# Weight loads of two blocks instead of four in a hybrid attention and FFN layer on one core

## The reference

```python
h = rmsnorm(x, attn_norm)
qkv = einsum('bsd,de->bse', h, w_in).reshape(B, S, 3, 16, 64)
q, k, v = rope(qkv[:, :, 0]), rope(qkv[:, :, 1]), qkv[:, :, 2]
o_moba = moba_attention(q[:, :, :8], k[:, :, :8], v[:, :, :8])      # 256 rows are one block: plain causal
o_dil  = dilated_mixture(q[:, :, 8:], k[:, :, 8:], v[:, :, 8:])     # windows 128/1, 512/4, 2048/16
mixed = concat([rmsnorm(o_moba, g1), rmsnorm(o_dil, g2)])
x = x + mixed @ w_out
h = rmsnorm(x, ffn_norm)
x = x + (silu(h @ w_gate) * (h @ w_up)) @ w_down                     # 1024 -> 2816 -> 1024
out = rmsnorm(x, final_norm)
```

## Time and profile before

| | |
|---|---|
| median of three runs | 304.27 us (304.18 to 304.38) |
| the profiled execution | 304.51 us |
| its span, first to last instruction | 302.7 us |
| TensorE busy | 294.1 us, 97% of the span |
| VectorE, ScalarE busy | 203.7 us, 166.9 us |
| granted TensorE clock | 0.994 of full speed |
| ring loads | 47 of 1 MB, 4.8 us from issue to landing (median) |
| DMA engines busy in the main queue | 57.5% |

### The profile page before, as it was taken

The page is one execution under the profiler, slowest core; times in us unless marked ns, Lnnn a source line. Parts: engine busy times, 40 slices in busy tenths (PEclk is TensorE's granted clock), DMA queues, the critical chain, the costliest instruction groups (busy, mean ns, idle before and its releaser), DMA issues.

```text
span 302.7 us, 4335 instructions
## 1 busy us (share of the span) xinstructions
PE 294.1 (97%) x1448; PEld 240.0 (79%) x1448; DVE 203.7 (67%) x332; ACT 166.9 (55%) x283; POOL 19.3 (6%) x29
## 2 busy tenths in 40 slices
PE   8999999999999899999999999999999999999992
PEld 4688877887788688888888888888888888888882
DVE  3889999977898589729755555637465655455454
ACT  4877775829686549816554445354363545444224
POOL 0011000030333120200000000000000000000010
PEclk9999999999999999999999999999999999999997
DMA  7998445851695535765876566575656564651003
GB/s 255 422 423 302 178 178 141 266 140 79 172 372 177 187 135 150 277 236 210 269 266 207 226 186 264 173 241 174 207 176 249 174 267 159 238 200 28 0 0 139
DMA packets 21757, 61.65 MB, mean 204 GB/s; under 512 B 2545, under 2 KB 13809, under 8 KB 15601
## 3 DMA queue, kind: packets, MB, share of 16 engines
q1 hardware_dynamic: 21312, 60.70, 57.5%
q10 hardware_dynamic: 432, 0.80, 0.7%
HBM read 54.67 MB, written 1.05 MB: 184 GB/s over the span
## 4 chain that ended last, share of the span: by engine, by line
PE 82%; ACT 5%; DMA 5%; issue 3%; DVE 2%; SPq 2%; POOL 0%; POOLq 0%; ACTq 0%; DVEq 0%
PE bank L437 27%; PE bank L439 26%; PE bank L438 26%; DMA raw<-in_weights 2%; DMA room<-in_first 2%; ACT w_hi L725 1%; SPq L403 1%; DMA room<-room 1%; ACT probs L820 1%; PE bank L464 1%; ACT vals L793 1%; PE bank L447 1%; DVE xs L1152 0%; ACT o_hi L836 0%; DVE w_lo L939 0%
## 5 line engine op out<-in xcount | busy, mean ns | idle before, releaser
L725 ACT ACTIVATE w_hi<-raw 128x1024 fp32r<-128x1024 f32 x94 | 98.0, 1056 | 81.2 <-PE bank L439 72.2
L939 DVE TENSOR_TENSOR w_lo<-raw,w_hi 128x1024 fp32r<-128x1024 f32 x94 | 112.3, 1217 | 17.1 <-ACT w_hi L725 15.7
L437 PE MATMUL bank<-w_hi,x_hi 128*128 128x512 f32 x270 | 106.8, 396 | 0.6 <-DVE w_lo L967 0.6
L439 PE MATMUL bank<-w_hi,x_lo 128*128 128x512 f32 x270 | 105.2, 390 | 0.0
L438 PE MATMUL bank<-w_lo,x_hi 128*128 128x512 f32 x270 | 105.2, 390 | 0.0
L437 PEld LDWEIGHTS bank<-w_hi,x_hi 128*128 128x128 f32 x270 | 50.7, 188 | 12.3 <-DVE w_lo L967 1.4
L439 PEld LDWEIGHTS bank<-w_hi,x_lo 128*128 128x128 f32 x270 | 50.7, 188 | 10.6
L438 PEld LDWEIGHTS bank<-w_lo,x_hi 128*128 128x128 f32 x270 | 50.7, 188 | 10.1
L437 PE MATMUL bank<-w_hi,h_hi 128*128 128x512 f32 (+1 forms) x82 | 31.6, 385 | 0.0
L439 PE MATMUL bank<-w_hi,h_lo 128*128 128x512 f32 (+1 forms) x82 | 31.5, 384 | 0.0
L438 PE MATMUL bank<-w_lo,h_hi 128*128 128x512 f32 (+1 forms) x82 | 31.5, 384 | 0.0
(11 more groups left out here) (101 smaller groups left out, 245.6 us busy)
## 6 DMA issues: line engine op xcount, KB each, us to landing
raw<-in_weights SPq DMA_DIRECT2D x47, 1024.0 KB, 4.8
room<-room SPq DMA_DIRECT2D x88, 64.0 KB, 2.1
room<-in_first SPq DMA_DIRECT2D x3, 384.0 KB, 5.1
room<-in_first SPq DMA_DIRECT2D x1, 1024.0 KB, 7.5
xs<-in_x SPq DMA_DIRECT2D x2, 512.0 KB, 9.3
out<-rot SPq DMA_DIRECT2D x3, 256.0 KB, 2.0
room<-in_first SPq DMA_DIRECT2D x1, 640.0 KB, 8.6
vals<-in_final_norm ACTq DMA_DIRECT2D x1, 512.0 KB, 7.2
```

What stands on the lines that cost most here:

```text
L437: pe.matmul(dst, a_hi, w1, start=first, stop=False)
L439: return pe.matmul(dst, a_lo, w1, start=False, stop=last)
L725: act.activation(w_hi[:, slot:slot + 2, :], raw[:, slot:slot + 2, :], ACT.Copy).then_inc(hi_ready, 1)
L939: dve.tensor_tensor(w_lo[:, slot:slot + 2, :], raw[:, slot:slot + 2, :], w_hi[:, slot:slot + 2, :].bitcast(f32), ALU.subtract).then_inc(lo ...
```

## The change

`quad` becomes `pair`: each load brings two blocks, 512 KB, as 128 rows of 4 KB that lie 8 KB apart in memory. There are six semaphores `raw_full`, one for each pair of slots. SP issues a pair when VectorE has finished with its own two slots: the first half waits for one `lo_ready` less than the quad did, the second half for the same count as the quad. The 47 ring loads become 94. The places of the other DMAs between them stay, behind both halves. The last loads of the six at the start no longer count on a semaphore of the ring but on their own. `split_hi` waits for the pair's semaphore, with the number of loads worked out by `ring_loads` (slots of the first four pairs have had one load fewer, since the first eight blocks don't pass through `raw`).

```diff
-        raw_full = [sem(f"raw_full{i}") for i in range(NQ)]
+        raw_full = [sem(f"raw_full{i}") for i in range(RING // 2)]
...
-        in_first = [raw_full[blocks[-1] // QUAD] if blocks[-1] % QUAD == QUAD - 1 else sem(f"in_first{i}")
-                    for i, (row_blocks, blocks) in enumerate(FIRST_LOADS)]
+        in_first = [sem(f"in_first{i}") for i in range(len(FIRST_LOADS))]
...
-            def quad(q, pos):
-                sp.dma_start(raw[:, pos * QUAD:(pos + 1) * QUAD, :].rearrange("p b n -> p (b n)"),
-                             weights[bass.ds(q - FIRST_QUADS, 1), :, :].rearrange("q p n -> (q p) n")).then_inc(raw_full[pos], 16)
+            def pair(q, pos, h):
+                first = 2 * h
+                sp.dma_start(raw[:, pos * QUAD + first:pos * QUAD + first + 2, :].rearrange("p b n -> p (b n)"),
+                             weights[bass.ds(q - FIRST_QUADS, 1), :, first * NB:(first + 2) * NB]
+                             .rearrange("q p n -> (q p) n")).then_inc(raw_full[2 * pos + h], 16)
...
-            quad(2, 2)
+            pair(2, 2, 0)
+            pair(2, 2, 1)
             sp.dma_start(tab[:, 0:C_MASK], table[:, 0:C_MASK]).then_inc(in_tab, 16)
-            sp.wait_ge(lo_ready, 2)
-            quad(NQ, 0)
+            for h in range(2):
+                sp.wait_ge(lo_ready, h + 1)
+                pair(NQ, 0, h)
...
             def ring_quad(r, pos):
-                sp.wait_ge(lo_ready, r * (RING // 2) + (2 * pos + 2 - RING // 2))
-                quad(r * NQ + pos, pos)
+                for h in range(2):
+                    sp.wait_ge(lo_ready, r * (RING // 2) + (2 * pos + h + 1 - RING // 2))
+                    pair(r * NQ + pos, pos, h)
...
             for q in range(BLOCKS // RING * NQ, BLOCKS // QUAD):
-                sp.wait_ge(lo_ready, 2 * q - 4)
-                quad(q, q % NQ)
+                for h in range(2):
+                    sp.wait_ge(lo_ready, 2 * q + h - 5)
+                    pair(q, q % NQ, h)
...
+            def ring_loads(p):
+
+                return 16 * (p // (RING // 2) + (0 if p % (RING // 2) < SINGLES // 2 else 1))
...
             def split_pair(p):
-                q = p // 2
-                if p < RING // 2:
-                    split_hi(2 * p, q, 16, None)
-                else:
-                    split_hi(2 * p % RING, q % NQ, 16 * (q // NQ + 1), 2 * p - 10)
+                split_hi(2 * p % RING, p % (RING // 2), ring_loads(p), 2 * p - 10 if p >= RING // 2 else None)
...
-                        q = (HI0 + m) // 2
-                        split_hi(2 * (HI0 + m) % RING, q % NQ, c * 16 + 16 * (q // NQ),
+                        p = HI0 + m
+                        split_hi(2 * p % RING, p % (RING // 2), c * 16 + (ring_loads(p) - 16),
                                  c * STEP_BLOCKS + (2 * (HI0 + m) - 10 - STEP_BLOCKS))
```

More of the change, by code:

```diff
@@ L378, in _ @@
             for pos in range(1, NQ):
-                sp.wait_ge(lo_ready, 2 * pos + 2)
-                quad(NQ + pos, pos)
+                for h in range(2):
+                    sp.wait_ge(lo_ready, 2 * pos + h + 1)
+                    pair(NQ + pos, pos, h)
             sp.dma_start(tab[:, C_MASK:C_END], table[:, C_MASK:C_END]).then_inc(in_mask, 16)
             def ring_quad(r, pos):
-                sp.wait_ge(lo_ready, r * (RING // 2) + (2 * pos + 2 - RING // 2))
-                quad(r * NQ + pos, pos)
+                for h in range(2):
+                    sp.wait_ge(lo_ready, r * (RING // 2) + (2 * pos + h + 1 - RING // 2))
+                    pair(r * NQ + pos, pos, h)
             def place_squares(c):
@@ L717, in _, with split_hi @@
             act.activation(warm_out[:, 0:1], warm[:, 0:1], ACT.Exp)
-            def split_hi(slot, pos, quad_round, done):
-                if quad_round is not None:
-                    act.wait_ge(raw_full[pos], quad_round)
+            def ring_loads(p):
+                return 16 * (p // (RING // 2) + (0 if p % (RING // 2) < SINGLES // 2 else 1))
+            def split_hi(slot, pos, loads, done):
+                act.wait_ge(raw_full[pos], loads)
                 if done is not None:
```

## The result

The changed kernel takes 305.18 us, the median of 12 runs from 304.27 to 306.54, against 304.27 us before (12 runs, 304.08 to 304.82). The ratio is 1.0031, with a 95% interval of 1.0019 to 1.0042: slower by 0.9 us, beyond the forecast's range. The runs also spread three times as far, though the kernel before itself later spread from 303.78 to 305.44 on another chip (35 runs).

The account below looks back on a forecast made before the run. TensorE, busy 294.1 of 302.7 us, was taken as the bound. Start, loop, issue and VectorE counted 0 and rows ahead of tile 11 +0.1, so 304.27 became 304.4 us, with a range of 303.7 to 305.0.

Parts of the forecast that it names:

- the bound and the place: TensorE bounds the kernel; the change comes near only its 0.92 us wait at `values` of tiles 10 and 11.
- The packets: Ring loads ahead of tile 11: shorter rows cost 0.08 us a quad, between 0 and 0.25, counted as +0.1 us.
- Half a load lands sooner: Ring loads: 512 KB lands in 2.9 us; ScalarE's longest load wait ends some 2 us sooner, worth 0 at tile 10.
- 47 more DMA instructions: SP's issue of DMAs: hidden in its waits, 0 to +0.65 us later at tile 11's issue.
- a later issue of tile 11 is hidden by a shorter landing: Tile 11's last placement DMA: time behind the ring load hides up to 1.86 us of later issue; counted 0, at most 0.65.
- VectorE: VectorE's work before tile 10: disturbed moves might give back or lose 0.7 us; taken at 0.
- rival B: Wait at 100.9 us shrinks as placements pass sooner or VectorE regains 0.7 us: 303.7 us, chance 0.10.
- Rival A: SP between 93.96 and 97.5 us: tile 11's DMAs go out and end 0.65 us later; 305.0 us, chance 0.16.
- `values` past 101.5: Sign of a slower kernel: `values` of tiles 10 and 11 start later than 101.5 us, against 100.92 before.
- Rival C: Ring loads in the loop stop overlapping, each paying its fixed part: 65 us more, 370 us, chance 0.01.

Follow-up runs that it names:

- the changed kernel again: The changed kernel with nothing altered, run once more for a second profile: two runs, 305.64 and 307.14 us.

## Why the prediction was wrong

Right were the bound and the place. TensorE waits three times, nowhere for a split from the ring; the FFN loop turn stays at 16.3 us; ScalarE's waits for loads fall from 8.8 to 2.6 us, though those for TensorE rise only from 72.2 to 73.0, where as much was forecast as the others fall; tile 11 is the exposed spot. What failed is how much reaches it.

*The step "The packets" failed.* It had a row cost its bytes plus 0.010 us, +0.1 us for a quad, from placements whose source is on the chip, and let that go straight to tile 11. As engine time the term was within its bound of 0.25: by the shares of the main queue, 57.5% of 302.7 us before and 60.2% of 303.6 after, the 47 quads cost 8.7 us more, 0.19 each, and by 58.6% of 302.8 us for 4 KB rows in one DMA 0.07 each. But what reaches TensorE is the landing, and there the runs showed something that the sum had no term for: the source address. Tile 11's last DMA lands in 4.47 us in place of 3.86, +0.6 us where +0.1 stood. Of that the contiguous pairs alone would have made -0.8 (3.08 us), and the stride +1.4. The two loads of (5, 1) tell it in each profile: the second half lands 4.5 to 4.6 us after its issue when contiguous, 5.3 to 6.6 when strided. From 95 to 98 us strided pairs move 184 to 257 GB/s, contiguous ones 295 and 302, whole loads of 1 MB 235 to 283. Bounds on a kind of read that the trace doesn't have should have been wider.

*The step "Half a load lands sooner" failed in size.* A straight line from 2.0 to 4.8 us gave 2.9; measured is 5.2, outside both ends. ScalarE's wait ended at 83.2 us, not near 82. The 2.0 us were those of a store of another kind, and the median in the queue includes what stands ahead.

*The step "47 more DMA instructions" was half right.* Its tally of the pushes, 0.65, 1.3 and 1.95 us, left 1.3 us of SP's pause. It took an issue as 0.63 us whatever the queue holds. With six DMAs where there were five, tile 8's took 1.0 us longer, the longest one 1.32 us, and the pause was gone. Kernels with the added DMAs around tile 8 all show this to a degree, from 2.73 us (contiguous pairs, tile 11 first) over 3.10 (the changed kernel again) to 4.52 (only (5, 1) whole), and whole loads there give 2.49 to 2.52; by what limit the issue is held back was not tried. That a later issue of tile 11 is hidden by a shorter landing, as the prediction had it, came out for half a us in both profiles of the added DMAs with hardly any bytes. Behind strided pairs it did not: in the second profile of the changed kernel 0.7 us came on top of a landing of 4.60.

*VectorE* did win time back, as rival B had it: tile 10 was turned at 91.0 us (90.30 + 0.70), 0.5 sooner once the shift of the start is taken off. It was worth nothing, since SP was busy until 91.4.

Rival A named the right place and half of the cause. In the first profile tile 11 was not issued later, it landed later; in the second it was both. Its price of +0.75 us and 305.0 us is close to what came, in part by luck, since the stride wasn't in it, and its test, `values` past 101.5, was met. It deserved more than 0.16: a place with no slack, a change that touches the queue ahead of it, and two unmeasured prices, both of which could only go one way by much. Rival C did not happen as a whole: pairs overlap, and the loop hides their slowness.

Left open: why strided loads land later though the engines are busy no longer, and why the profile with padding between the rows doesn't show it at tile 11; why contiguous pairs are faster than a quad (0.9983 against 1, and 1.0005 for the quad of 4 KB rows); the 0.6 us that the median of the kernel with tiny added DMAs shows and its profiles don't; and that with (3, 1) to (4, 0) in pairs besides (5, 1) the time is 305.05 (1.0024) and without them 304.74 (1.0008), whose intervals overlap.

## What to carry to other kernels

Before cutting a load in two, ask what each half reads: halves by columns of a row-major piece read with gaps, and the layout in memory should be cut along with the load. Where one queue carries both bulk loads and small transfers that an engine waits for, find the small transfer with no slack and put it ahead of the load; that was worth 0.7 us here (304.33 to 303.58) and needed nothing else. Slack between DMA issues in a trace is no promise for a kernel with more DMAs: with one added to each load the same four issues took 2.7 to 4.5 us in place of 2.5, whatever the added one carried.

## What the runs showed of the hardware

- 512 KB in 4 KB rows land in 4.3 us (median in this kernel) from contiguous memory and in 5.2 us with an 8 KB pitch; 1 MB in 8 KB rows in 4.8. The Trainium skill, "DMA: Bandwidth & Descriptors", section "Anatomy of one DMA — SWDGE (gpsimd) path", has a fit for GpSimd's DMAs, 2.0 us and the bytes at 436 GB/s, which as an estimate gives 3.2 us for 512 KB. The runs here, with DMAs issued by SP behind others, are above that.
- A load into 64 partitions at a time lands in 7.2 us for 512 KB and made the kernel 8% slower. The same page of the Trainium skill, section "The descriptor swizzle", has, for a transfer to 128 partitions, the lower 64 written through one half of the ports and the upper 64 through the other. A rate of 205 to 237 GB/s at a share of 0.9, against 393 at 1.06 in the kernel before, would go with half of the ports at a time, but no run here separates ports from engines.
- Issuing a DMA of 64 KB took SP 0.60 us as a rule and up to 1.32 us in the changed kernel, where more DMAs were queued.
- Strided and contiguous pairs keep the DMA engines busy for the same share of the span (60.2 and 60.8%), although the strided ones land later.
- The first multiplications are uneven from one execution to the next: in the profiles the wait that ends near 8 us varies between 0 and 1.1 us in kernels whose first loads are identical, and nothing of a faster start is kept where `values` waits for a landing. How much of the spread of the runs comes from it was not measured.
